# Mixture of experts on one core: experts ranked by token count, tiles of 64, 32 and 32 slots in a pass

## The reference, cut to what matters

```
scores = sigmoid(x @ router);  sel = scores + router_bias
... top 4 of 8 groups, then top 8 experts:  combine (tokens x 64 experts)
h = silu(einsum('btd,edf->btef', x, w_gate)) * einsum('btd,edf->btef', x, w_up)
routed = einsum('btef,efd->btd', h * combine[..., None], w_down)
return routed + (silu(x @ ws_gate) * (x @ ws_up)) @ ws_down
```

## Time and profile before

| | us |
|---|---|
| median of three runs | 1690.45 (1688.8 to 1691.01) |
| the profiled execution | 1692.0 |
| its span, first to last instruction | 1690.2 |
| PE busy (matmuls) | 1544.3 (91%) |
| PEld busy (weight loads) | 801.3 (47%) |
| DVE busy | 527.8 (31%) |
| ACT busy | 389.9 (23%) |
| read from HBM | 503.02 MB, 299 GB/s over the span |

### The profile page before, as it was taken

How to read it: one execution, slowest core, us unless ns; L and a number is a source line. 1 busy time by engine, 2 the same in 40 slices (tenths; PEclk the granted TensorE clock), 3 DMA queues, 4 the chain that set the end, 5 groups by cost and what they waited for, 6 DMA issues and landing times.

```text
span 1690.2 us, 24406 instructions
## 1 busy us (share of the span) xinstructions
PE 1544.3 (91%) x9667; PEld 801.3 (47%) x9667; DVE 527.8 (31%) x1183; ACT 389.9 (23%) x762; POOL 41.1 (2%) x17
## 2 busy tenths in 40 slices
PE   3899878799999999999977987699999999999995
PEld 1777654654444444444433454464444444444442
DVE  1123455613223232322313242522323232232322
ACT  0201631312222222222221042412222222222221
POOL 0002020100000000000000000100000000000000
PEclk9899989899999999999987998899999999999998
DMA  8795856259999999999944222629999999999971
GB/s 328 292 342 177 308 206 258 116 216 383 383 377 392 376 392 376 383 384 378 392 155 158 100 75 92 287 104 365 390 375 390 378 383 384 378 393 373 394 289 49
DMA packets 101940, 505.81 MB, mean 299 GB/s; under 512 B 16201, under 2 KB 20870, under 8 KB 51974
## 3 DMA queue, kind: packets, MB, share of 16 engines
q1 hardware_dynamic: 100160, 501.32, 74.7%
q10 hardware_dynamic: 1414, 2.78, 0.5%
q0 software_dynamic: 320, 1.06, 0.2%
HBM read 503.02 MB, written 2.11 MB: 299 GB/s over the span
## 4 chain that ended last, share of the span: by engine, by line
PE 85%; DVE 6%; ACT 3%; issue 2%; ACTq 0%; DVEq 0%
PE PS L562 83%; PE PS L724 1%; DVE diag L1250 1%; DVE x L1254 1%; DVE W L1381 0%; DVE W L1495 0%; DVE W L1472 0%; DVE hT L1230 0%; DVE sst L1646 0%; DVE W L1372 0%; DVE diag L1664 0%; PE PS L910 0%; ACT junk L1025 0%; ACT W L1069 0%; ACT W L1070 0%
## 5 line engine op out<-in xcount | busy, mean ns | idle before, releaser
L562 PE MATMUL PS<-ring,W 128*64 128x512 f32 (+1 forms) x3200 | 735.4, 597 | 10.3 <-DVE W L1386 9.9
L562 PEld LDWEIGHTS PS<-ring,W 128*64 128x64 f32 (+1 forms) x3200 | 228.6, 138 | 412.0 <-issue 401.4
L562 PE MATMUL PS<-W 128*128 128x128 bf16 (+5 forms) x3102 | 409.6, 266 | 10.4 <-ACT W L1100 3.4
L562 PEld LDWEIGHTS PS<-W 128*128 128x128 bf16 (+2 forms) x3102 | 234.7, 102 | 138.2 <-issue 65.8
L1447 DVE TENSOR_TENSOR W<-PS,W 128x512 f32<-128x512 f32 x130 | 89.9, 692 | 191.0 <-ACT W L1098 191.0
L562 PE MATMUL PS<-W,junk 128*128 128x128 bf16 x1040 | 143.0, 219 | 2.2 <-DVE W L1408 1.3
L1441 DVE COPY W<-PS 128x512 f32<-128x512 f32 x65 | 45.0, 692 | 296.2 <-PE PS L562 296.2
L1098 ACT CAST W<-PS 128x512 bf16<-128x512 f32 x130 | 76.2, 586 | 244.2 <-PE PS L562 244.2
L562 PE MATMUL PS<-ring,hT 128*128 128x512 f32 x256 | 114.5, 610 | 2.4 <-issue 1.6
L1424 DVE SCALAR_TENSOR_TENSOR W<-W,PS 128x256 f32<-128x256 f32 x65 | 31.2, 480 | 242.8 <-ACT W L1085 242.8
L1085 ACT ACTIVATE W<-PS 128x256 f32<-128x256 f32 x65 | 25.0, 384 | 311.3 <-PE PS L562 311.3
(11 more groups left out here) (223 smaller groups left out, 850.3 us busy)
## 6 DMA issues: line engine op xcount, KB each, us to landing
ring<-in_moe_w_gate SPq DMA_DIRECT2D x130, 1024.0 KB, 8.7
ring<-in_moe_w_up SPq DMA_DIRECT2D x130, 1024.0 KB, 10.7
ring<-in_moe_w_down SPq DMA_DIRECT2D x130, 1024.0 KB, 8.3
ring<-in_mod_w SPq DMA_DIRECT2D x32, 1152.0 KB, 11.5
ring<-in_mod_w SPq DMA_DIRECT2D x16, 768.0 KB, 14.9
ring<-in_attn_w_qkv SPq DMA_DIRECT2D x12, 768.0 KB, 6.5
ring<-in_lru_w_in SPq DMA_DIRECT2D x8, 960.0 KB, 15.3
ring<-in_lru_w_out SPq DMA_DIRECT2D x4, 1024.0 KB, 8.3
```

What stands on the lines that cost most here:

```text
L562: return eng.matmul(out, lhsT, rhs, start=first, stop=last, skip_group_check=True)
```

## The change

Experts 0 to 3 stay first, with 64 slots each. The other 60 are ranked by their number of tokens, on the chip, and served in a fixed pattern of passes by rank: kind A has two experts of 64 slots; kind B one of 64 and two of 32; kind D one of 96 (a tile of 64 and one of 32) and one of 32. A layer has 2 passes A and three rounds of `BABABABD`: 26 passes. Ranks 4 to 6 have 96 slots, the next 30 ranks 64, the last 27 32. Experts with more tokens than slots get extra items of 64 slots, in pairs, as before.

A block of 32 slots is a column of the tables, four columns a pass, 104 in all. Each expert's key is 64 times its count plus 63 minus its number (the fixed four get larger keys); a matmul spreads the keys, a comparison and a sum give the rank, a comparison with a constant row gives the column matrix `M`, and a matmul with it the experts' numbers by column. SyncE waits for them once (`ids_ready`) and reads them into registers ahead of each pass's loads. Each pass that frees slots of the ring has its own pair of waits; the loops of the five engines now have a round of eight passes as their body on TensorE and SyncE, and two passes on ScalarE and VectorE. Within a pass, both scatters stand ahead of turn_hidden. The extra loads wait for the last pass.

```diff
+STATIC = 4
+BODY = "BABABABD"
+ROUNDS = 3
+PASSES = 2 + ROUNDS * len(BODY)
+COLS = 4 * PASSES
+ITEMS = COLS + 2 * XITEMS
+SUBS = {"A": (0, 0, 1, 1), "B": (0, 0, 1, 2), "D": (0, 0, 0, 1)}
...
+        def lanes(kind, first):
+
+            cut = {"A": (0, 64, 128), "B": (0, 64, 96, 128), "D": (0, 64, 96, 128)}[kind]
+            return [(lo, hi - lo, (first + SUBS[kind][lo // 32]) % RING) for lo, hi in zip(cut, cut[1:])]
...
+                eng.wait_ge(s.ids_ready, L + 1)
+                with eng.Fori(0, ROUNDS) as it:
+                    for p, taken in enumerate(FREED):
+                        done = it * len(BODY) + (L * PASSES + p + 1)
+                        experts = [eng.value_load(xtab[0:1, bass.ds(it * 4 * len(BODY) + (2 * 4 + ID_COL[m]), 1)],
+                                                  min_val=0, max_val=E - 1) for m in taken]
+                        eng.wait_ge(s.gu_done, done)
+                        for m, e in zip(taken, experts):
+                            load_gate_up(ring[:, m % RING], a["moe_w_gate"][L, e], a["moe_w_up"][L, e],
+                                         slot_sem(m % RING))
+                        eng.wait_ge(s.down_done, it * 2 * len(BODY) + 2 * (L * PASSES + p + 1))
...
-                eng.wait_ge(s.down_done, 2 * ((L + 1) * PAIRS - 1))
+                eng.wait_ge(s.down_done, 2 * (L + 1) * PASSES)
...
                 for k in range(KD):
-                    for e in range(2):
-                        w = ring[:, places[e], 0:4096].rearrange("p (m k f) -> p k m f", m=2, k=KD)
-                        ins = mm(PS[e * 64:(e + 1) * 64, 6, :].rearrange("p (m f) -> p m f", m=2),
-                                 xg[:, k, e * 64:(e + 1) * 64], w[:, k], k == 0, k == KD - 1)
+                    for lo, n, q in places:
+                        w = ring[:, q, 0:4096].rearrange("p (m k f) -> p k m f", m=2, k=KD)
+                        ins = mm(PS[lo:lo + n, 6, :].rearrange("p (m f) -> p m f", m=2),
+                                 xg[:, k, lo:lo + n], w[:, k], k == 0, k == KD - 1)
...
+                def one_pass(j, i, places, turn, item, first=False, more=True):
+                    if not first:
+                        pass_gate_up(j, places, turn)
+                        for st in range(NS):
+                            scatter(s, j - 1, st, (i + 1) % 2)
+                    turn_hidden(s, j)
+                    if more:
+                        eng.wait_ge(s.hT_ready, j + 1)
+                        gather(s, j + 1, S[(i + 1) % 2])
+                    pass_down(j, places, turn)
+                    if more:
+                        turn_slots(s, item + 4, j + 1, (i + 1) % 2)
...
-                for e in range(2):
-                    eng.tensor_reduce(wslot[e * 64:(e + 1) * 64, 0:1], PS[e * 64:(e + 1) * 64, 7, 3 * e:3 * e + 3],
+                for e in range(4):
+                    eng.tensor_reduce(wslot[e * 32:(e + 1) * 32, 0:1], PS[e * 32:(e + 1) * 32, 7, 3 * e:3 * e + 3],
                                       AX, ALU.add).then_inc(sg_.wT_ready, 1)
...
+                eng.wait_ge(s.plan_pe, PLAN_PE["keys_spread"] + 5 * L)
+                dve.keep(eng.tensor_scalar(above[0:E, :], PS[0:E, 5, 64:128], nb[0:E, 0, 8:9], None, ALU.is_gt))
+                dve.settle()
+                dve.keep(eng.tensor_reduce(nb[0:E, 0, 9:10], above[0:E, :], AX, ALU.add))
+                dve.settle()
+                eng.tensor_scalar(M[0:E, :], con[0:E, C_RANK:C_RANK + COLS], nb[0:E, 0, 9:10], None, ALU.is_equal)\
+                   .then_inc(s.plan_dve, 1)
+                eng.wait_ge(s.plan_pe, PLAN_PE["ids_done"] + 5 * L)
+                eng.tensor_copy(xtab[0:1, 0:COLS], PS[0:1, 5, 128:128 + COLS]).then_inc(s.ids_ready, 1)
```

More of the change, by code:

```diff
@@ L46, with column_ranks @@
 XITEMS = T * 8 // SLOTS
-ITEMS = E + XITEMS
-PAIRS = E // 2
+STATIC = 4
[5 more added lines that the diff above has]
+SUBS = {"A": (0, 0, 1, 1), "B": (0, 0, 1, 2), "D": (0, 0, 0, 1)}
+FIRST = [sum(SUBS[q][-1] + 1 for q in BODY[:i]) for i in range(len(BODY))]
+PER_ROUND = sum(SUBS[q][-1] + 1 for q in BODY)
+def column_ranks():
+    big, mid = iter(range(STATIC, STATIC + ROUNDS)), iter(range(STATIC + ROUNDS, E))
+    lanes = [[(0, 2), (1, 2)], [(2, 2), (3, 2)]]
+    n_mid = ROUNDS * (BODY.count("B") + 2 * BODY.count("A"))
+    small = iter(range(STATIC + ROUNDS + n_mid, E))
+    for _ in range(ROUNDS):
+        for kind in BODY:
+            if kind == "A":
+                lanes.append([(next(mid), 2), (next(mid), 2)])
+            elif kind == "B":
+                lanes.append([(next(mid), 2), (next(small), 1), (next(small), 1)])
+            else:
+                lanes.append([(next(big), 3), (next(small), 1)])
+    return [(rank, block) for places in lanes for rank, blocks in places for block in range(blocks)]
 EPS = 1e-6
@@ L245, in trunk @@
         wsum = c(NS, 2)
-        nb = c(1, 8)
-        M, bM = c(32), c(32)
+        nb = c(1, 16)
+        M, Mx, bM = c(COLS), c(XITEMS), c(XITEMS)
+        key, above = c(E), c(E)
+        xtab_place = c(COLS + XITEMS + 8)
         ppT, combT = c(T), c(T)
@@ new lines, in one_round @@
+                def one_round(it, last):
+                    for i, kind in enumerate(BODY):
+                        used_ = range(FIRST[i], FIRST[i] + SUBS[kind][-1] + 1)
+                        one_pass(it * len(BODY) + (L * PASSES + 2 + i), i, lanes(kind, FIRST[i]),
+                                 [(m % RING, it * (PER_ROUND // RING) + (1 + m // RING)) for m in used_],
+                                 it * 4 * len(BODY) + 4 * (2 + i), more=not (last and i == len(BODY) - 1))
+                for i in range(2):
+                    one_pass(L * PASSES + i, i, lanes("A", 2 * i), [(2 * i, 0), (2 * i + 1, 0)], 4 * i, first=i == 0)
@@ L866, in moe @@
+                with eng.Fori(0, ROUNDS - 1) as it:
+                    one_round(it, False)
+                one_round(ROUNDS - 1, True)
                 for st in range(NS):
-                    scatter(s, (L + 1) * PAIRS - 1, st, 1)
+                    scatter(s, (L + 1) * PASSES - 1, st, 1)
                 xs = extra[L]
-                count = eng.value_load(xtab[0:1, 32:33], min_val=0, max_val=XITEMS)
+                count = eng.value_load(xtab[0:1, X_COUNT:X_COUNT + 1], min_val=0, max_val=XITEMS)
@@ L1518, in shared_hidden, with places, paired @@
                        .then_inc(s.sh_h, 1)
-                shared_hidden(0)
+                def places(first, end, sub):
+                    return posL[:, first + sub:end:2, :].rearrange("p e s -> p s e")
+                def paired(first, end):
+                    return lambda q: com3[:, :, first:end, q].rearrange("p s (e two) -> p s e two", two=2)
                 eng.wait_ge(s.ranks_done, L + 1)
@@ new lines, in moe @@
+                eng.wait_ge(s.plan_pe, PLAN_PE["extra_done"] + 5 * L)
+                dve.keep(eng.tensor_copy(xtab[0:1, X_IDS:X_IDS + XITEMS], PS[0:1, 5, 256:288]))
+                table = PS[:, 5, 288:416].rearrange("p (s w x) -> p w s x", s=NS, w=2)
+                for sub in range(2):
+                    dve.keep(eng.tensor_scalar(places(COLS, ITEMS, sub), table[:, 0], -1.0 - 32 * sub, None, ALU.add))
+                dve.settle()
+                weight_parts(paired(COLS, ITEMS), bc(table[:, 1], 3, 2),
+                             com_rest[:, :, 0:2 * XITEMS].rearrange("p s (e two) -> p s e two", two=2))\
+                    .then_inc(s.xtable_ready, 1)
```

248 lines of the change are left out of this document (129 added, 119 removed).

## The result

The changed kernel takes 1946.26 us (median of 4 runs, 1945.31 to 1949.6), the kernel before 1689.85 us in the same comparison: ratio 1.152, 95% interval 1.150 to 1.154. The forecast was 1950 us. The profiled execution took 1949.6 us, its span 1947.8.

What follows compares the result with a forecast made beforehand. TensorE was taken to bound the MoE stages, the DMA close behind. +126.3 us per layer, twice +252.6, plus +6.3 for the extra pair: +258.9 on 1692.0, less 1.5 for the median, 1950 us; range 1600 to 1985.

Steps and rivals of the forecast that it cites:

- The bound: MoE stages: a pass over two experts takes 16.44 us on TensorE, 15.0 us on the DMA close behind.
- Widths side by side: Gate and up and down of B and D passes: alternating 64 and 32 columns stops TensorE, +13.7 us a pass.
- four prices: B or D pass: widths overlap, 0; overlap lost without toll, +9.9; stop per width change, +13.7; matmul passes alternate too, +17.5 us.
- the sign: Gate and up in B passes: weight loads in single pairs, idle about 0.6 us before each change of width.
- first rival: MoE passes: different widths on disjoint columns run together, DMA becomes the bound; 1613 us, range 1595 to 1650, chance 0.29.
- the case 0.48: Likeliest case: every change of width waits for the array, +13.7 us per B or D pass; own range 1900 to 1990.
- third rival: B and D passes: overlap of widths lost but no toll per change, +9.9 us a pass; 1836 us, chance 0.08.
- Order inside a pass: Second scatter ahead of the turn leaves ScalarE's copy uncovered before the gather: +0.68 us in each pass but the last.
- Start: Ranking plan, table matmuls and waits ahead of and behind the first gate and up: +2.8 us per layer, bounds 0 and 8.
- SyncE: Load queue: waiting for ids_ready and up to three register loads per pass cost nothing, hidden in 7 us of slack.
- the later wait: Extra pair's loads wait for the last down instead of the one before: +6.3 us, in layer 1 alone.
- Weights are in time: B and A alternating: five experts take 47.9 us on TensorE and 37.4 us on the DMA, so weights never hold it up.

Runs made afterwards that it cites:

- e6_turn_between: The changed kernel with the turn of hidden rows put back between the two scatters: 1933.61 us.
- e1_all32: The changed kernel with passes B and D cut into four tiles of 32 columns: 1698.79 us, ratio 1.006 to the kernel before.

## Why the prediction was right, point by point

- *The bound.* TensorE bounded the MoE stages before, and bounds them after, as forecast.
- *Widths side by side.* This was the step with a choice of four prices (0, +9.9, +13.7 and +17.5 us a pass), and 13.7 was taken because each change of width in the trace of before showed the stop, though always on shared columns. Measured: +13.2, in the changed kernel and in the kernel before with mixed tiles. A change costs 0.14 us on average where 0.15 and 0.17 were read from rows 3 and 4, and the idle time on the load path is 0.81 to 0.84 us where 0.6 was named as the sign; 30 passes of 30.37 us instead of 30.8 are 13 us. The Trainium skill's rule by which the forecast and not the first rival comes out (page "TensorEngine Tiling (Array Packing)", section Key Properties: a change of tiling mode drains TensorE, a change of tile alone doesn't) holds here for disjoint columns too: the runs with one width throughout have no stop between tiles, those with two have one at each change. The prediction said that its trace did not show this for disjoint columns, and gave the case 0.48; the range, 1600 to 1985, would also have held the third rival and most of the first. So it is the 13.2 us, and not the range, that bear the mechanism out.
- *Order inside a pass.* Forecast 0.68 us a pass, measured 0.71 where it is put back alone. That undoing it is worth 35 us would have been wrong: 12.6.
- *Start.* Forecast 2.8 us a layer, measured 3.3 and 2.6.
- *SyncE.* The register loads hide, as forecast. "Any slot may hold the last experts" was wrong; the last pass always has slots 2 and 3. The price of the later wait was mis-sized too, 9.2 us for 6.3: the wait is 1.1 us longer, and the clock behind it was left out.
- *Left out.* The jump back over a long body: 8.7 us, of which 5.4 are idle time (3.9 and 1.5) and 3.2 the clock that fell behind it in layer 0.
- *DMA.* "Weights are in time" was right for this kernel, but not by the argument given, five experts' bytes against five experts' time. What decides is the chain from the end of one B's gate and up to the next B: 31.2 to 31.4 us in which 11 loads pass one queue. With 15.9 us of gate and up that is a period of 47.1 to 47.3 us, just under the kernel's 47.5; in run e6_turn_between TensorE alone would need 46.1, and the period is 47.0 to 47.7.
- *First rival.* Its condition, all tiles at once, was made true in run e1_all32 by giving them one width, and its time, 1613 us, was too low by 86. Its range, 1595 to 1650, did not hold it either. It had the waits at 3 us before B and named the clock without a price; the clock costs 2.6 us each, and through the ring it is the DMA that loses them.
- *Errors that cancelled.* 13 us too much for the changes of width, against 8.7 for the jump back and 3 for the extra pair. The median is within 4 us of the forecast partly by that.

## What to carry to other kernels

Tiles of 64 and of 32 columns did not run at once in any run here, tiles of one width did. So make a 64-slot lane beside 32-slot lanes two tiles of 32 columns; their extra instructions were free here. When passes are made cheaper, look at the chain of loads that one pass's end releases and the next pass waits for, not at the mean share of the DMA. A wait of 4 us cost more than itself here, since the clock fell behind it, and where the work behind it releases the next loads, the loss goes round again: either spread the demand so that there is hardly a wait (1631.65 us), or spread it less and keep TensorE busy through the wait that is left (1626.93 us).

## What the runs showed that was not expected

- A jump back over eight passes on TensorE: 3.9 us of idle time and 3.2 us of a lowered clock in the first layer, 1.5 us in the second; 2.3 to 3.7 us idle and a lowered clock behind it in two other runs; written out in line, nothing.
- After a wait of 4.1 us with nothing to do, 4 us at a granted clock of 0.50 and 2 us at 0.72; with matmuls whose results nobody uses in the wait, gate and up takes 7.07 us instead of 9.62, and the kernel 26 us less.
- Four tiles of 32 columns with twice the instructions are not slower than two of 64: 16.42 us a pass for 16.44.
- The DMA moved 410 to 413 GB/s over 400 us at a share of 1.00, where the two kernels compared had 383 and 310.
